# Two transformer blocks on one core: first stage reordered, with the second group's sums loaded sooner and sums and splits alternating on VectorE

## The reference, cut to what matters

```
cs = silu(c)
mod = cs @ w_ada[l] + b_ada[l]                 # w_ada is 2048 x 12288
sh1, sc1, gt1, sh2, sc2, gt2 = split(mod, 6)
h = _rmsnorm(x, g_pre_mix[l]) * (1.0 + sc1) + sh1
proj = h @ w_in[l]                             # h is 256 x 2048, w_in 2048 x 11344
...                                            # attention, output products, feed-forward
x = second_block(x, ...)                       # the same kind of work again
```

## Time and profile before

| | |
|---|---|
| runs of the kernel before, us | 2582.1, 2576.09, 2584.29 (median 2582.1) |
| the profiled execution, us | 2584.16 |
| its span, us | 2582.4 |
| mean granted TensorE clock | 0.995 |
| TensorE busy | 2546.8 us (99%) |
| VectorE busy | 1732.4 us (67%) |
| ScalarE busy | 1202.8 us (47%) |

### The profile page before, as it was taken

One profiled execution on the slowest core, in us unless ns is written; L12 is line 12 of the kernel. 1 busy time (PEld: TensorE's weight loads), 2 busy tenths in 40 slices (PEclk: granted clock), 3 DMA queues, 4 the chain that ended last, 5 costly groups with the idle time before them and its releaser, 6 DMA issues.

```text
span 2582.4 us, 30501 instructions
## 1 busy us (share of the span) xinstructions
PE 2546.8 (99%) x12354; PEld 2117.9 (82%) x12354; DVE 1732.4 (67%) x2329; ACT 1202.8 (47%) x1735; POOL 6.4 (0%) x16
## 2 busy tenths in 40 slices
PE   8999999999999999999999999999999999999998
PEld 4787788888887888888888888878788888888887
DVE  6886988788886866556556565546665575664665
ACT  4444445444446434435434465455564344443443
POOL 0000000000000000000000000000000000000000
PEclk9999999999999999999999999999999999999999
DMA  9985276588985785555555545534545555555553
GB/s 399 366 322 186 98 261 264 183 338 313 345 338 221 263 304 192 199 187 187 203 180 192 204 167 180 195 114 147 196 173 200 182 188 203 180 195 196 180 198 145
DMA packets 78748, 567.11 MB, mean 220 GB/s; under 512 B 8800, under 2 KB 8928, under 8 KB 10256
## 3 DMA queue, kind: packets, MB, share of 16 engines
q1 hardware_dynamic: 77472, 558.09, 58.9%
q0 software_dynamic: 1136, 7.07, 0.7%
HBM read 563.02 MB, written 2.10 MB: 219 GB/s over the span
## 4 chain that ended last, share of the span: by engine, by line
PE 89%; DVE 7%; ACT 2%; DMA 1%; issue 1%; DVEq 0%; SPq 0%; ACTq 0%
PE ps L1121 20%; PE ps L1124 20%; PE ps L1122 20%; PE ps L1165 15%; PE ps L1170 8%; DVE wl L1860 3%; DMA raw<-stream_in 1%; DVE ACC L1894 1%; DVE ACC L1881 1%; PE ps L1405 1%; PE ps L1106 1%; ACT wh L1465 1%; PE ps L1381 0%; PE ps L1237 0%; PE ps L1207 0%
## 5 line engine op out<-in xcount | busy, mean ns | idle before, releaser
L1860 DVE TENSOR_TENSOR wl<-raw,wh 128x1024 fp32r<-128x1024 f32 x837 | 986.8, 1220 | 564.3 <-ACT wh L1465 563.9
L1465 ACT ACTIVATE wh<-raw 128x1024 fp32r<-128x1024 f32 x837 | 838.2, 1049 | 715.2 <-PE ps L1124 580.5
L1121 PE MATMUL ps<-wh,U 128*128 128x512 f32 x1376 | 538.8, 392 | 0.0
L1124 PE MATMUL ps<-wl,U 128*128 128x512 f32 x1376 | 537.1, 390 | 1.1 <-DVE wl L1860 1.1
L1122 PE MATMUL ps<-wh,U 128*128 128x512 f32 x1376 | 536.1, 390 | 0.0
L1165 PE MATMUL ps<-HT,wh 128*128 128x512 f32 x1792 | 449.8, 393 | 0.0
L1121 PE MATMUL ps<-wh,HT 128*128 128x512 f32 x1080 | 433.8, 402 | 5.4 <-DVE M L2228 3.4
L1124 PE MATMUL ps<-wl,HT 128*128 128x512 f32 x1080 | 425.4, 394 | 2.4 <-DVE wl L1860 2.3
L1122 PE MATMUL ps<-wh,HT 128*128 128x512 f32 x1080 | 423.8, 392 | 0.0
L1165 PEld LDWEIGHTS ps<-HT,wh 128*128 128x128 f32 x1792 | 323.0, 189 | 58.3 <-DVE M L2265 0.2
L1124 PEld LDWEIGHTS ps<-wl,U 128*128 128x128 f32 x1376 | 258.4, 188 | 58.0 <-DVE wl L1860 4.2
(11 more groups left out here) (284 smaller groups left out, 1473.4 us busy)
## 6 DMA issues: line engine op xcount, KB each, us to landing
raw<-stream_in SPq DMA_DIRECT2D x524, 1024.0 KB, 4.8
M<-rows_in POOLq DMA_DIRECT2D x6, 1024.0 KB, 5.6
M<-stream_in SPq DMA_DIRECT2D x3, 1024.0 KB, 10.9
y_out<-X SPq DMA_DIRECT2D x3, 512.0 KB, 2.6
X<-x_in SPq DMA_DIRECT2D x1, 1024.0 KB, 5.4
X<-x_in SPq DMA_DIRECT2D x2, 512.0 KB, 15.3
raw<-stream_in SPq DMA_DIRECT2D x1, 640.0 KB, 7.2
raw<-stream_in SPq DMA_DIRECT2D x1, 512.0 KB, 3.4
```

The source lines that it names most:

```text
L1121: e.matmul(o, ah, H[:, c:c + bw], start=k == k0, stop=False)
L1124: ins = e.matmul(o, ah, L[:, c:c + bw], start=False, stop=end)
L1465: e.activation(H, raw[place[n][0]][:, c:c + w], ACT.Copy).then_inc(*hi.tick(p))
L1860: e.tensor_tensor(L, raw[place[n][0]][:, c:c + w], H.bitcast(F32), ALU.subtract).then_inc(*lo.tick(p))
```

## The change: what it does

- **Stream.** The first two of group 1's four events come ahead of kB@0 (they were behind the first chunk of vB@0, as 8 and 9; they are now 6 and 7, in buffers that nobody has used yet). The second half of x is loaded in two transfers with event 4 between them; before, both came ahead of event 4. In group 3 the two events in a row move from behind vB@1's first chunk to behind vA@0's third.
- **Plain chunks.** qi@0 and the first chunk of vB@0 are plain; qB@0 is split now.
- **TensorE's start.** 24 matmuls of constants (128x128, as the four that were there already) are put ahead of everything else on TensorE.
- **First stage.** Group 1 is summed ahead of the first chunk of vB@0, not in the middle of it. The splits of qB@0 and kB@0 are placed earlier on ScalarE.
- **By turns.** In `run`, for "s" events: ScalarE's copies come first as before; on VectorE one sum and one subtraction take turns, and what is left of the sums follows. Ahead of the last chunk of an @1 slab the subtractions come first, and the sums follow only after three of the slab's four additions into M.
- **One accumulator in group 2** (ACC2 now holds only 512 columns, for group 1), which halves its column-sum matmuls.

```diff
-PLAIN = ("qi@0", "qB@0")
+PLAIN = (("g", "qi@0", 0), ("g", "vB@0", 0))
...
-    out += group_events(0) + chunks("qi@0") + chunks("qB@0") + chunks("kB@0") + chunks("vB@0", 0, 1) + group_events(1)
+    second = group_events(1)
+    out += group_events(0) + chunks("qi@0") + chunks("qB@0") + second[:2] + chunks("kB@0") + second[2:] + chunks("vB@0", 0, 1)
     beside(chunks("vB@0", 1) + chunks("kA@0") + chunks("vA@0", 0, 2), group_events(2), (1, 2, 2, 2, 1))
-    beside(chunks("vA@0", 2) + chunks("kA@1") + chunks("vB@1") + chunks("kB@1", 0, 1), group_events(3), (1, 1, 1, 1, 1, 2, 1))
+    beside(chunks("vA@0", 2) + chunks("kA@1") + chunks("vB@1") + chunks("kB@1", 0, 1), group_events(3), (2, 1, 1, 1, 1, 1, 1))
...
-                sums += ada(nx)
+                if events[nx][0] == "s":
+                    rows += [(nx, j) for j in range(2)]
+                    if events[nx][2] == 7:
+                        sums.append(nx)
+                else:
+                    sums += ada(nx)
                 nx += 1
+            if rows:
+                late_rows = rows if EARLIER.get(name) and i + 1 == total else []
+                for j in range(2):
+                    split_piece(nx, j, only=("ACT",))
+                lows = [] if hold and own else list(parts[nx])
+                for m, j in () if late_rows else rows:
+                    add("DVE", "ada", m, j)
+                    if lows:
+                        add("DVE", "split", lows.pop(0))
+                for p in lows:
+                    add("DVE", "split", p)
+                if late_rows:
+                    def rest_of_rows(late_rows=late_rows):
+                        for m, j in late_rows:
+                            add("DVE", "ada", m, j)
+                    hooks[1, 0] = rest_of_rows
...
+    def whole(n, between=None):
...
+    add("constants", 24)
     add("xsquare", 0)
...
-    native(4)
+    native(chunk("qi@0"))
+    native(chunk("vB@0"))
...
-    native(5)
+    split(chunk("qB@0"))
...
-    for n in (10, 11):
+    second = [events.index(e) for e in group_events(1)]
+    for n in second[:2]:
         add("ada", n)
+    whole(chunk("qB@0"), lambda: split(chunk("kB@0")))
+    for n in second[2:]:
+        add("ada", n)
+    whole(chunk("kB@0"))
     for j in range(2):
-        split_piece(12, j, only=("ACT",))
+        split_piece(chunk("vB@0", 1), j, only=("ACT",))
+    add("DVE", "split", parts[chunk("vB@0", 1)][0])
+    colsum(second[3])
+    add("xhalves", 1)
+    add("DVE", "split", parts[chunk("vB@0", 1)][1])
+    for t in range(2):
+        add("xq", 2, t)
     for t in range(2):
         for b in range(2):
-            add("bank", "vB@0", parts[7], t, b, True, False)
-            if (t, b) == (1, 0):
-                colsum(11)
-                add("xhalves", 1)
+            add("bank", "vB@0", parts[chunk("vB@0")], t, b, True, False)
...
-        return [ACC[:, 0:w], ACC2[:, 0:w]] if g in (1, 2) else [ACC[:, 0:256 if g == 0 else w]]
+        return [ACC[:, 0:w], ACC2[:, 0:w]] if g == 1 else [ACC[:, 0:256 if g == 0 else w]]
...
         for n, (off, w) in enumerate(offs):
-            if n == 4:
-                for j in range(2):
-                    a = slice(1024 * j, 1024 * j + 1024)
-                    e.dma_start(X[:, 1, a], x_in[0, 128:256, a]).then_inc(x_landed[1 + j], 16)
+            if n in (4, 5):
+                a = slice(1024 * (n - 4), 1024 * (n - 4) + 1024)
+                e.dma_start(X[:, 1, a], x_in[0, 128:256, a]).then_inc(x_landed[n - 3], 16)
```

More of the change, by code:

```diff
@@ L336, in native @@
             parts[n].append(len(pieces))
[L337 removed]
+            pieces.append({"n": n, "ks": ks, "width": 1024, "w": 1024, "c": 1024 * (ks[0] % 2), "slot": None})
     def split(n, room=None):
@@ L398, in run @@
                 split(n + j)
-            nx, sums = n + many, []
+            nx, sums, rows = n + many, [], []
             while nx < len(events) and events[nx][0] != "g":
@@ L611, in sums, with chunk @@
         add("rowvec", n)
+    def whole(n, between=None):
+        name = events[n][1]
+        for t in range(2):
+            for b in range(2):
+                add("bank", name, parts[n], t, b, True, True)
+                evac(name, t, b)
+            if between and t == 0:
+                between()
+        at["done"] = parts[n][-1]
+    def chunk(name, i=0):
+        return events.index(("g", name, i))
+    add("constants", 24)
     add("xsquare", 0)
@@ L643, in work_order @@
     at["done"] = parts[4][-1]
[L644 to L654 removed]
+    second = [events.index(e) for e in group_events(1)]
+    for n in second[:2]:
         add("ada", n)
+    whole(chunk("qB@0"), lambda: split(chunk("kB@0")))
+    for n in second[2:]:
+        add("ada", n)
+    whole(chunk("kB@0"))
     for j in range(2):
[L657 removed]
+        split_piece(chunk("vB@0", 1), j, only=("ACT",))
[3 more added lines that the diff above has]
+    add("DVE", "split", parts[chunk("vB@0", 1)][1])
+    for t in range(2):
+        add("xq", 2, t)
     for t in range(2):
         for b in range(2):
[L660 to L669 removed]
+            add("bank", "vB@0", parts[chunk("vB@0")], t, b, True, False)
+    at["done"] = parts[chunk("vB@0")][-1]
+    at["pos"] = chunk("vB@0", 1)
     def third_pair():
@@ L1021, in read_last @@
     def read_last(n):
-        if events[n][1] in PLAIN:
+        if events[n] in PLAIN:
             return gemm(("piece", last_piece[n]))
@@ L1101, in bank_mm @@
                     e.wait_ge(*s(k))
-            for p in ps if name in PLAIN else ():
-                n, k, c = pieces[p]["n"], pieces[p]["ks"][0], pieces[p]["c"] + 512 * b
-                e.wait_ge(*(floated_v if k else floated)(("hf", k, t)))
-                e.wait_ge(*arrived(n))
-                ins = e.matmul(o, HF[:, k, 128 * t:128 * t + 128], raw[place[n][0]][:, c:c + 512], start=k == 0, stop=k == 1)
-                done = [("piece", p)] if (t, b) == (1, 1) else []
-                if done or k == 1:
-                    ins.then_inc(*gemm.tick(*done, *([(name, t, b)] if k == 1 else [])))
-            for p in ps if name not in PLAIN else ():
+            for p in ps:
+                ks = pieces[p]["ks"]
+                if pieces[p]["slot"] is None:
+                    n, k, c = pieces[p]["n"], ks[0], pieces[p]["c"] + 512 * b
+                    e.wait_ge(*(floated_v if k else floated)(("hf", k, t)))
+                    e.wait_ge(*arrived(n))
+                    ins = e.matmul(o, HF[:, k, 128 * t:128 * t + 128], raw[place[n][0]][:, c:c + 512], start=k == 0,
+                                   stop=last and k == k1 - 1)
+                    keys = [("piece", p)] if (t, b) == (1, 1) else []
+                    if last and k == k1 - 1:
+                        keys.append((name, t, b))
+                    if keys:
+                        ins.then_inc(*gemm.tick(*keys))
+                    continue
                 H, L = piece_memory(p)
-                ks = pieces[p]["ks"]
                 for j, k in enumerate(ks):
@@ L1860, in split, with ada @@
             e.tensor_tensor(L, raw[place[n][0]][:, c:c + w], H.bitcast(F32), ALU.subtract).then_inc(*lo.tick(p))
-        def ada(n):
+        def ada(n, only=None):
             kind, g, i = events[n]
@@ L1870, in ada @@
                 for j, k in enumerate(ks):
+                    if only not in (None, j):
+                        continue
                     a, r = both[k % len(both)], raw[place[n][0]][:, step * j + r0:step * j + r0 + w]
```

22 lines of the change are left out of this document (1 added, 21 removed).

## The result

The changed kernel is slower: 2588.95 us median (2586.93 to 2591.54, 10 runs), against 2582.7 us (2576.09 to 2586.19, 10 runs) of the kernel before, taken beside it. The ratio is 1.0026, with a 95% interval of 1.0017 to 1.0035. In a second set it was 1.0030 (1.0020 to 1.0041). The profiled execution took 2588.02 us, its span is 2586.2.

A forecast was written before the change was run, and what follows sets the result against it. TensorE bounds the kernel, busy 99% of the span. Running offsets of +1.5, +1.5, +1.7 and finally -2.4 us against the span 2582.4 gave 2580.0, or 2579.7 us on the median; range 2573 to 2586.

The forecast's parts named there:

- Start: Up to TensorE's first product: x's last part lands behind event 4, product at 24.4 instead of 22.92, +1.5 us; constants 0.
- To the end of vB@0: First product to vB@0's end: old waits go, others come, next chunk starts at 60.0 against 58.60; running delay stays +1.5 us.
- rival C: Clock falls a third time, between 44.3 and 47.2, where TensorE waits then does only column sums: +2.5, 2582.2 us; chance 0.20.
- Group 2: VectorE stalls 5.3 us for event 17's copy; sums end at 85.0, not 80.89; TensorE waits 3.3 us.
- Clock and column sums: From 85.05, halved column sums and half clock behind the wait; next chunk ends at 99.8 against 98.06, running delay +1.7 us.
- Group 3: 2.78 us wait for M and 3.4 us of half clock go; column sums at 137.0 against 139.42, running total -2.4 us.
- Behind it: After group 3: nothing changes (0); group 4's turns are covered by VectorE's idle time, otherwise at most a microsecond's wait.
- The median: Step from profiled span to typical run: profiled execution took 2584.16, 2.1 above the median 2582.1; forecast span 2580.0 became 2579.7.
- a wait like that of 2.78: Assumption that TensorE's forecast 3.3 us wait before group 2's column sums brings half clock, as the 2.78 us wait had.

The follow-up runs named there:

- group 2's sums first: The kernel after, with VectorE doing the sums of group 2's first half ahead of the subtraction of the low halves; 2585.26 us, ratio 1.0012 to before.
- group 4 as before: The kernel after, with group 4's sums and splits in the order of the kernel before (no turns); 2587.19 us, ratio 1.0022 to before.
- x late: The kernel before, with only x's last part issued behind weight event 4, as in the kernel after; 2583.15 us, ratio 1.0004 to before.

## Why the prediction was wrong

It said 2579.7 us, no change; it came to 2588.95. In the profile's own terms it said a span of 2580.0, and 2586.2 was measured: 6.2 us too little, and 3 more on the median. TensorE was 1.3 us behind the forecast where qB@0 starts, 3.4 at the chunk behind vB@0's plain one, 3.85 at group 2's column sums and 3.7 at group 3's, and it lost 2.3 more behind 150 us: 6.0 of the 6.2. Three terms of the sum were too small: the start, the stretch up to the end of vB@0, and "behind it nothing". The 3 us on the median are the step from one profiled execution to a typical run, which I had made as if both kernels' executions stood to their medians alike.

*Start* (+1.5): the delay itself was 0.76 and 1.24 us in the two profiles of the kernel after, for x came with the loads somewhat earlier. What failed is that the term held a delay alone and took the full clock behind it for granted. The clock fell at 21.8, 0.6 us after TensorE had begun to wait, and was at half until 28.6, so that in the first profile qB@0 starts at 33.74, 1.3 us behind the forecast 32.4. Whether the constants, which I took at 0, have a part in this fall is open: in the kernel before they cost nothing (0.9996), and the kernel after without them has no fall there, but times that don't settle it.

*To the end of vB@0* (+1.5): this was rival C, given 0.20. TensorE waited 0.8 us and did column sums, and at 49.2 the clock fell over the plain chunk. Ten of the eleven traces with the new first stage show this fall, beginning at 44.8 to 50.4, and none of the seven with the old one. My argument against it was that the same column sums at 46.97 had no fall behind them; but there was no wait ahead of those, and the condition that I had named myself is the pair of both. The next chunk started at about 63.4 and not at 60.0; 2.1 us of these 3.4 arose here.

*Group 2*: the mechanism was right, and so was TensorE's wait: 3.3 us forecast, 3.44 measured. VectorE's stall was 7.37 and not 5.3, since the copy came 3.4 us later (64.13, forecast 60.7) and VectorE 1.3 later (forecast 56.6). Group 2 was summed at 88.9 instead of 85.05, nearly all of it carried over from the two steps ahead; TensorE was late by the same delay, so its own wait stayed as forecast. In the run with group 2's sums first they are through 2.8 us earlier, which is what this order costs. That was in my sum, as a price; what I hadn't done was to ask whether the rest of the sum could pay for it.

The forecast of 0.1 us for each sum that follows another in one accumulator held: 5.30 against 4.87 for four. The Trainium skill, "VectorE: DVE Perf Modes", section "The DRAIN you can't avoid", says of a row of copies that a semaphore on each of the VectorE operations costs nothing over one at the end; here the measurement decides against taking that to mean that one accumulator is as fast as two.

*Clock and column sums*: the half clock behind the wait came (90.1 to 96.9), the halved column sums too.

*Group 3* (-2.4): right. No wait for M, no half clock at 128, and waits for low halves of 0.62 at 127.12 and 0.63 at 138.97, where I had 0.8 and 0.95; a wait of 0.49 for HT at 103.31 wasn't in my replay. From group 2's column sums to group 3's, 58.5 us before and 51.8 now, with 51.95 forecast.

*Behind it* (0): wrong. I had written "at most a wait of a microsecond" and looked at VectorE's idle time as a mean. There were two waits, 1.35 and 0.62 us; from one matmul's start to the next they make 1.75 and 1.01 where 0.23 is usual, 2.3 us in all. With group 4 as before both are gone, and "rest" is 2.2 lower.

*The median*: this is the part that I took for bookkeeping. The profiled execution of before had 17.1 us of half clock ahead of 150 us, worth 8.5. Traces of kernels that differ from before in one edit have 3.4 or 6.8 us (the constants 3.4, x late 6.8, one accumulator 3.4), and the mean clock of the 130 runs, 0.9968, says the same against that execution's 0.995. So not every run of the kernel before can have both of the falls from which I let the change win; which ones it has is known of one execution only. The kernel after has 0.9960 in both sets, and both its traces have 17 us. Of 7.1 us between the means (2588.9 and 2581.8), 2.1 are half clock and 5.0 the rest. The idle stretch at the end takes up to 1.5 us more of "lost" in the trace of before (9.4 us of half clock against 6.4), so the share of half clock during work may be up to 3.6.

One reading of mine was wrong though it did no harm here: "a wait like that of 2.78 was followed by half clock". By the earlier trace rows the clock is at half from 127.6, and TensorE stood until 128.26: it fell during the wait, not behind it.

Why only the new first stage brings the fall at about 47 in so many of its traces is not shown beyond what precedes it, 0.8 us of wait and 1.9 of column sums. A version with the new first stage without that wait wasn't made.

## What to carry to other kernels

Putting two kinds of work by turns on an engine helps only if both can run then: each turn that waits for another engine's late copy also holds up the work behind it that was ready, here 7.37 us of it. A wait that is removed uncovers the next one in the same queue; read what stands in front of the instruction that TensorE will need next (here x's turn behind four sums, which a pair of numbers settled: 2.49 us of wait went, worth 3 us by the medians and within the noise of the times). Where the clock changes from run to run, one profile's half clock isn't a gain to be collected: hold it against the mean clock of all runs before it goes into a sum.

## What the runs showed of the hardware

The times of one kernel go with its mean granted clock. Of 130 runs of the kernel before, the 29 with a clock of 0.998 took 2578.1 us on the mean, the 44 with 0.997 took 2581.7, the 34 with 0.996 2584.0 and the 12 with 0.995 2585.2. From 0.998 to 0.995 that is 7.1 us, and 0.003 of 2582 us is 7.7. So most of the difference between runs of one kernel is half clock, and the clock belongs beside every time.

A wait of the same length came with half clock in one execution and not in another. The wait for M at about 124 to 128 was 2.78 us in the kernel before, with half clock from 127.6 on; with the constants (2.79) and with one accumulator (2.78) the clock fell in it too. With x late it was 2.79 us, and a window of TensorE there has the full clock:

```profile
128.00:131.40 3.40, 3.01 (x13) 1.00 0.96 361
```

Group 2's column sums had a wait of 0.72 us ahead of them in the kernel with one accumulator, about as in the kernel before (0.61), and the window shows full clock where before had half. Here the work isn't quite the same, since the column sums themselves are halved:

```profile
82.50:85.90 3.40, 3.37 (x23) 1.00 1.01 422
```

So the wait for M came with a fall in three traces of four, and doesn't decide it. The kernel after is the other case: its falls came at the same instructions in both of its traces. Nor is the length of the wait all: at 21.8 the clock fell when TensorE had stood for 0.6 us of its 2.50, after a stretch of small matmuls.
